# First attention's scores as two full-array passes over stacked parts, with the parts made by ScalarE and VectorE

## What is computed

```python
q = rmsnorm(q.reshape(B, S, N_HEADS, HEAD_DIM), q_gain)
k = rmsnorm(k.reshape(B, S, N_HEADS, HEAD_DIM), k_gain)
...
s = jnp.einsum('bqhd,bkhd->bhqk', qb, kb).astype(jnp.float32) * scale + bias
s = jnp.where(valid[None, None], s, NEG_INF)
p = jax.nn.softmax(s, axis=-1)
return jnp.einsum('bhqk,bkhd->bqhd', p.astype(vb.dtype), vb)
```

## Time and profile before

| | |
|---|---|
| median of three runs | 1531.12 us |
| the profiled execution's own time | 1531.12 us |
| its span, first to last instruction | 1529.3 us |
| TensorE busy | 1508.3 us (99%) |
| VectorE, ScalarE, GpSimd busy | 744.7, 578.6, 125.0 us |
| granted TensorE clock, mean | 0.999 |

### The profile page before, as it was taken

One profiled execution on the slowest core, in us unless ns is written; L12 is line 12 of the kernel. 1 busy time (PEld: TensorE's weight loads), 2 busy tenths in 40 slices (PEclk: granted clock), 3 DMA queues, 4 the chain that ended last, 5 costly groups with the idle time before them and its releaser, 6 DMA issues.

```text
span 1529.3 us, 18943 instructions
## 1 busy us (share of the span) xinstructions
PE 1508.3 (99%) x7006; PEld 1233.0 (81%) x7006; DVE 744.7 (49%) x1068; ACT 578.6 (38%) x941; POOL 125.0 (8%) x102
## 2 busy tenths in 40 slices
PE   8999999999999999999999999999999999999998
PEld 7888888887885688888888887887788888888886
DVE  5444433347345655444323456676557542244434
ACT  5323221224325533322212255666745443124322
POOL 0000000002005120000000024256000000000000
PEclk9999999999999999999999999999999999999999
DMA  6333353334221133333333334520233332233222
GB/s 188 97 99 95 98 138 100 97 97 122 86 83 47 56 110 92 96 99 95 98 97 97 96 97 112 178 83 29 83 100 111 107 96 96 97 96 96 96 97 97
DMA packets 247833, 151.19 MB, mean 99 GB/s; under 512 B 18128, under 2 KB 230752, under 8 KB 247520
## 3 DMA queue, kind: packets, MB, share of 16 engines
q1 hardware_dynamic: 234432, 143.67, 31.9%
q10 hardware_dynamic: 13344, 6.75, 1.6%
HBM read 144.10 MB, written 5.78 MB: 98 GB/s over the span
## 4 chain that ended last, share of the span: by engine, by line
PE 91%; DVE 3%; ACT 3%; issue 1%; DMA 1%; SPq 0%; DVEq 0%; ACTq 0%
PE bank L389 29%; PE bank L393 28%; PE bank L392 28%; DVE w_low L1196 1%; PE bank L2151 1%; PE bank L2203 1%; DMA region_f<-in_x 1%; PE bank L2162 1%; ACT w_high L655 0%; PE bank L2375 0%; PE bank L2090 0%; DVE region L1540 0%; DMA rope_w<-rope_y 0%; PE bank L2235 0%; PE bank L2214 0%
## 5 line engine op out<-in xcount | busy, mean ns | idle before, releaser
L389 PE MATMUL bank<-region,w_high 128*128 128x512 f32 (+2 forms) x1492 | 585.3, 392 | 4.9 <-DVE w_low L1196 1.4
L393 PE MATMUL bank<-region,w_low 128*128 128x512 f32 (+2 forms) x1492 | 579.4, 388 | 0.0
L392 PE MATMUL bank<-region,w_high 128*128 128x512 f32 (+2 forms) x1492 | 579.0, 388 | 0.0
L1196 DVE TENSOR_TENSOR w_low<-w_raw,w_high 128x1024 fp32r<-128x1024 f32 (+1 forms) x259 | 334.0, 1295 | 149.9 <-ACT w_high L655 145.9
L655 ACT CAST w_high<-w_raw 128x1024 fp32r<-128x1024 f32 (+1 forms) x259 | 265.8, 1027 | 257.6 <-DMA w_raw<-in_ffn_w_down 107.2
L389 PEld LDWEIGHTS bank<-region,w_high 128*128 128x128 f32 (+1 forms) x1492 | 279.6, 187 | 65.6 <-DVE w_low L1196 3.8
L393 PEld LDWEIGHTS bank<-region,w_low 128*128 128x128 f32 (+1 forms) x1492 | 279.5, 187 | 59.2
L392 PEld LDWEIGHTS bank<-region,w_high 128*128 128x128 f32 (+1 forms) x1492 | 279.7, 187 | 56.0
L389 PE MATMUL bank<-w_high,region 128*128 128x512 f32 x416 | 164.3, 395 | 2.4 <-ACT x L978 1.5
L393 PE MATMUL bank<-w_high,region 128*128 128x512 f32 x416 | 162.2, 390 | 0.0
L392 PE MATMUL bank<-w_low,region 128*128 128x512 f32 x416 | 161.9, 389 | 0.0
(11 more groups left out here) (265 smaller groups left out, 1188.8 us busy)
## 6 DMA issues: line engine op xcount, KB each, us to landing
w_raw<-in_ffn_w_down SPq DMA_DIRECT2D x48, 512.0 KB, 3.9
w_raw<-in_ffn_w_gate SPq DMA_DIRECT2D x44, 512.0 KB, 3.8
w_raw<-in_ffn_w_up SPq DMA_DIRECT2D x44, 512.0 KB, 3.8
w_raw<-in_w_in SPq DMA_DIRECT2D x40, 512.0 KB, 3.9
w_raw<-in_w_up SPq DMA_DIRECT2D x32, 512.0 KB, 4.0
w_raw<-in_w_down SPq DMA_DIRECT2D x32, 512.0 KB, 3.3
w_raw<-in_w_out SPq DMA_DIRECT2D x16, 512.0 KB, 3.9
region_f<-in_x SPq DMA_DIRECT2D x4, 512.0 KB, 7.5
```

Source lines behind the costliest of these rows:

```text
L389: mm = pe.matmul(out, a_hi, b_hi, start=start, stop=False)
L392: pe.matmul(out, a_hi, b_lo, start=False, stop=False)
L393: return pe.matmul(out, a_lo, b_hi, start=False, stop=stop)
L1196: last = dve.tensor_tensor(piece(w_low[b % RING]), piece(w_raw[b % RING]), piece(w_high[b % RING]).bitcast(F32), ALU.subtract)
```

## The change

The scores of a window are computed by two fp32r passes for each head, each over all 128 rows. The stationary operand is a stacked query tile: the high part of the head's queries in its own 64 partitions (HOME) and the low part in the other 64 (OTHER). The first pass multiplies it with a tile that holds the high part of the keys in both halves, the second with a tile that holds the low part of the keys in the home half and zeros in the other. For each pair of heads ScalarE makes 6 copies of 64x512 (2 of queries, 4 of keys), VectorE 4 subtractions of 64x512, GpSimd 2 memsets of 64x512. Pairs 2 and 3 use the same tiles as 0 and 1, and their high parts wait for the scores of the pair two before. GpSimd's four memsets stand ahead of its pool work. The head norms are spread in the order 0, 4, 1, 5, 2, 6, 3, 7. The semaphores of the second block's parts are shared with the new ones and counted on.

```diff
@@ ScalarE, after the casts of the value blocks
+            def a_query_parts(p):
+                act.wait_ge(qk_full_ready, 2 * p + 1)
+                if p >= 2:
+                    act.wait_ge(a_score, 8 * (p - 1))
+                for c in range(2):
+                    last = act.copy(a_query(p, c)[HOME[c], :], over[1][HOME[c], p, :])
+                last.then_inc(query_hi, 1)
+            def a_key_parts(p):
+                act.wait_ge(qk_full_ready, 2 * p + 2)
+                if p >= 2:
+                    act.wait_ge(a_score, 8 * (p - 1))
+                for c in range(2):
+                    act.copy(a_key(p, c)[HOME[c], :], over[1][HOME[c], 4 + p, :])
+                    last = act.copy(a_key(p, c)[OTHER[c], :], over[1][HOME[c], 4 + p, :])
+                last.then_inc(key_hi, 1)
+            for p in range(2):
+                a_query_parts(p)
+                a_key_parts(p)
@@ ScalarE, loop, after the exponentials and before the copy of sums, pooled_hi and split_hi
+                if w in (4, 8):
+                    a_query_parts(w // 4 + 1)
+                if w in (5, 9):
+                    a_key_parts(w // 4 + 1)
@@ VectorE, head norms
+                j = HEAD_ORDER[i]
                 dve.wait_ge(h_bc, i + 1)
-                dve.scalar_tensor_tensor(over[1][:, i, :], qk_raw[:, i, :], qk_gain[:, i // 4:i // 4 + 1],
+                dve.scalar_tensor_tensor(over[1][:, j, :], qk_raw[:, j, :], qk_gain[:, j // 4:j // 4 + 1],
@@ VectorE, after the value tiles
+            def query_low_parts(p):
+                dve.wait_ge(query_hi, p + 1)
+                for c in range(2):
+                    last = dve.tensor_tensor(a_query(p, c)[OTHER[c], :], over[1][HOME[c], p, :],
+                                             a_query(p, c)[HOME[c], :].bitcast(F32), ALU.subtract)
+                last.then_inc(query_lo, 1)
+            def a_key_low_parts(p):
+                dve.wait_ge(key_hi, p + 1)
...
+                for c in range(2):
+                    last = dve.tensor_tensor(a_key_low(p, c)[HOME[c], :], over[1][HOME[c], 4 + p, :],
+                                             a_key(p, c)[HOME[c], :].bitcast(F32), ALU.subtract)
+                last.then_inc(key_lo, 1)
+            query_low_parts(0)
+            a_key_low_parts(0)
             u_tile(0, bank[5])
             for w in range(2 * HEADS):
                 p, q = divmod(w, TT)
+                if w in (1, 5, 9):
+                    query_low_parts(w // 4 + 1)
+                if w in (2, 6, 10):
+                    a_key_low_parts(w // 4 + 1)
@@ GpSimd, after the sum of squares
+            for p in range(2):
+                if p == 1:
+                    pool.wait_ge(qk_full_ready, 8)
+                for c in range(2):
...
+                    pool.memset(a_key_low(p, c)[OTHER[c], :].bitcast(F32), 0.0).then_inc(pads_in, 1)
@@ TensorE
-                pe.matmul(bank[6 + i % 2][:], head_select[:, P * i:P * (i + 1)], head_rows[:], start=True, stop=True).then_inc(h_bc, 1)
+                j = HEAD_ORDER[i]
+                pe.matmul(bank[6 + i % 2][:], head_select[:, P * j:P * (j + 1)], head_rows[:], start=True, stop=True).then_inc(h_bc, 1)
...
+                if q == 0:
+                    pe.wait_ge(query_lo, p + 1)
+                    pe.wait_ge(key_lo, p + 1)
+                    pe.wait_ge(pads_in, min(2 * p + 2, 4))
...
-                    pe.matmul(bank[4 + c][:, 0:n], over[1][rows_, p, q * P:(q + 1) * P], over[1][rows_, 4 + p, 0:n],
-                              start=True, stop=True).then_inc(a_score, 1)
+                    queries = a_query(p, c)[:, q * P:(q + 1) * P]
+                    pe.matmul(bank[4 + c][:, 0:n], queries, a_key(p, c)[:, 0:n], start=True, stop=False)
+                    pe.matmul(bank[4 + c][:, 0:n], queries, a_key_low(p, c)[:, 0:n], start=False, stop=True).then_inc(a_score, 1)
```

More of the change, by code:

```diff
@@ L121 @@
 SQ, _ = numbered([("m1", 8), ("f2", 8), ("m2", 16)])
+PARTS, _ = numbered([("a", 4), ("d", 4)])
+PADS, _ = numbered([("a", 4), ("d", 8)])
 SPREAD, _ = numbered([("f1", 1), ("m1", 1), ("f2", 1), ("m2", 1)])
@@ L340, in build, with a_query, a_key, a_key_low @@
         CONV_ORDER = (0, 2, 1, 3)
+        HEAD_ORDER = (0, 4, 1, 5, 2, 6, 3, 7)
+        A_QUERY = (((2, 4), (2, 5)), ((1, 9), (1, 10)))
+        A_KEY = (((2, 6), (2, 7)), ((1, 11), (1, 15)))
+        A_KEY_LOW = (((2, 16), (2, 17)), ((2, 13), (2, 14)))
+        def a_query(p, c):
+            return d_place(A_QUERY, p % 2, c)
+        def a_key(p, c):
+            return d_place(A_KEY, p % 2, c)
+        def a_key_low(p, c):
+            return d_place(A_KEY_LOW, p % 2, c)
         mv_plain = over[2][:].rearrange("p a b -> p (a b)")[:, 0:TT * MH * MV].rearrange("p (k h c) -> p k h c", k=TT, h=MH)
@@ L515, in build @@
         mv_ready = sem("mv_ready")
-        e_query_hi, e_query_lo, e_key_hi, e_key_lo, e_padded = (sem("d_" + n) for n in (
+        query_hi, query_lo, key_hi, key_lo, pads_in = (sem(n) for n in (
             "query_hi", "query_lo", "key_hi", "key_lo", "key_pads_zero"))
@@ L923, in d_query_hi @@
                     last = act.copy(d_query(h, c)[HOME[c], :], over[1][HOME[c], h, :])
-                last.then_inc(e_query_hi, 1)
+                last.then_inc(query_hi, 1)
             def d_key_hi(h):
@@ L929, in d_key_hi @@
                 if h == 2:
-                    act.wait_ge(e_key_lo, 2)
+                    act.wait_ge(key_lo, PARTS["d"] + 2)
                 if h == 3:
-                    act.wait_ge(e_query_lo, DH)
+                    act.wait_ge(query_lo, PARTS["d"] + DH)
                 for c in range(2):
@@ L935, in d_key_hi @@
                     last = act.copy(d_key(h, c)[OTHER[c], :], over[1][HOME[c], 4 + h, :])
-                last.then_inc(e_key_hi, 1)
+                last.then_inc(key_hi, 1)
             for i in range(8):
@@ L1536, in d_query_lo @@
             def d_query_lo(h):
-                dve.wait_ge(e_query_hi, h + 1)
+                dve.wait_ge(query_hi, PARTS["d"] + h + 1)
                 for c in range(2):
@@ L1541, in d_query_lo @@
                                              d_query(h, c)[HOME[c], :].bitcast(F32), ALU.subtract)
-                last.then_inc(e_query_lo, 1)
+                last.then_inc(query_lo, 1)
             def d_key_lo(h):
-                dve.wait_ge(e_key_hi, h + 1)
+                dve.wait_ge(key_hi, PARTS["d"] + h + 1)
                 if h == 2:
@@ L1549, in d_key_lo @@
                 if h == 3:
-                    dve.wait_ge(e_key_lo, 3)
+                    dve.wait_ge(key_lo, PARTS["d"] + 3)
                 for c in range(2):
@@ L1553, in d_key_lo @@
                                              d_key(h, c)[HOME[c], :].bitcast(F32), ALU.subtract)
-                last.then_inc(e_key_lo, 1)
+                last.then_inc(key_lo, 1)
             for i in range(6, 8):
@@ L1866, in _ @@
             sum_squares("m1")
+            pool.wait_ge(sq_added, SQ["m1"] + DT)
+            for p in range(2):
+                if p == 1:
+                    pool.wait_ge(qk_full_ready, 8)
+                for c in range(2):
+                    if p or c:
+                        pool.wait_ge(pads_in, 2 * p + c)
+                    pool.memset(a_key_low(p, c)[OTHER[c], :].bitcast(F32), 0.0).then_inc(pads_in, 1)
+            pool.wait_ge(pads_in, 4)
             for j in range(4):
@@ L1896, in _ @@
                 if h == 3:
-                    pool.wait_ge(e_key_lo, 3)
+                    pool.wait_ge(key_lo, PARTS["d"] + 3)
                 for c in range(2):
                     if h or c:
-                        pool.wait_ge(e_padded, 2 * h + c)
-                    pool.memset(d_key_low(h, c)[OTHER[c], :].bitcast(F32), 0.0).then_inc(e_padded, 1)
+                        pool.wait_ge(pads_in, PADS["d"] + 2 * h + c)
+                    pool.memset(d_key_low(h, c)[OTHER[c], :].bitcast(F32), 0.0).then_inc(pads_in, 1)
             def convolve(i):
@@ L2315, in d_scores @@
                 if q == 0 and c == 0:
-                    pe.wait_ge(e_query_lo, h + 1)
-                    pe.wait_ge(e_key_lo, h + 1)
-                    pe.wait_ge(e_padded, 2 * h + 2)
+                    pe.wait_ge(query_lo, PARTS["d"] + h + 1)
+                    pe.wait_ge(key_lo, PARTS["d"] + h + 1)
+                    pe.wait_ge(pads_in, PADS["d"] + 2 * h + 2)
                 if u >= 2:
```

5 lines of the change are left out of this document (2 added, 3 removed).

## The result

The kernel after takes **1550.11 us** (median of 4 runs, 1547.01 to 1551.12), the kernel before 1531.13 on the same chip: ratio 1.0118 with a 95% interval of 1.0106 to 1.0129 (ratios are given so below), 19.0 us slower. The forecast was 1541.0 with a range to 1546. The sign and the places of the waits were right; GpSimd's blocking and TensorE's clock were priced far too low. The profiled execution is the shortest of the four, 1547.01 us at a mean granted clock of 0.995; the other three had 0.991 to 0.993. So the trace explains 15.9 us of the 19.0.

What follows compares the result with a forecast made beforehand. The prediction took TensorE to bound the kernel (busy 99%, 91% of the chain). Loop waits of 11.0 plus 0.5 for GpSimd less 1.6 gained gave +9.9 us on 1531.12, so 1541.0, range 1534.5 to 1546.

Steps and rivals of the forecast that it cites:

- 1: scores of window 3: Before window 3's scores: VectorE's two key subtractions delay window 2's minima, with no cover; +1.4 us.
- 2: sums of window 5: Spreading the sums, window 5: query copies and subtractions lengthen the chain by 2.64 us against cover 0.85; +1.8 us.
- 3: scores of window 7: Before window 7's scores: ScalarE's four key copies delay its pool cast, then VectorE's subtractions and minima; dearest, +3.3 us.
- 4: sums of window 9: Spreading the sums, window 9: chain again 2.64 us longer against a cover of about 0.45; +2.2 us.
- TensorE's own gain: Score passes in the attention loop: new form gains 0.4 us a pair, 1.6 for four; bounds 1.0 and 2.6.
- Ahead of the loop: Parts made before the loop's first scores: cost nothing, with a cover of 1.3 us.
- The six places: Waits of TensorE at windows 3, 5, 7, 9, 11 and 12 from parts made inside the loop; 11.0 us together.
- I take 0.5 in all: Subtractions of windows 1 and 5 slowed beside GpSimd's additions: 0 to 0.6 us each of four, 0.5 taken in all.
- The rival: GpSimd blocks VectorE: four subtractions lose about a whole addition each, 4.4 us instead of 0.5, 1544.9; chance 0.10.
- The clock: Rival: clock falls in window 7's stall, next 3 to 5 us of TensorE work take twice as long, 1545; chance 0.10.
- Hiding: Rival: new ScalarE and VectorE work fits their idle time in the loop, leaving only TensorE's gain, 1529.5; chance 0.10.
- cheaper instructions: Rival: loop copies and subtractions overlap at some 0.5 and 0.6 us and covers recover, 1536.8; chance 0.15.

Runs made afterwards that it cites:

- e6_moved2: Changed kernel with its new copies and subtractions placed where engines idled, and pair 0's low part and the last key subtraction moved later; 1529.53 us.
- e10: Changed kernel without GpSimd's running sums, with 10, 10, 20 and 10 extra TensorE transposes fitted into four waits; 1541.13 us, ratio 1.0066.
- e1: Changed kernel with 26, 18, 12 and 16 extra TensorE transposes into a free bank during four waits; 1546.51 us, ratio 1.0104.
- e8_place1: Changed kernel with pair 1's four subtractions ahead of the loop instead of at the heads of windows 1 and 2; 1544.96 us, ratio 1.0083.
- e2_nopool: Changed kernel with GpSimd's running sums left out, a scaling of 8 columns in their place; 1543.54 us, ratio 1.0079.
- e3_short: Changed kernel with the copies and subtractions of pairs 2 and 3 cut to 8 of 512 columns; 1537.20 us, ratio 1.0042.

## Why the prediction was wrong, step by step

The array's work is the same in all these kernels but the one before, so the time from one window's first score pass to the next one's, less the same in e6_moved2, prices each place. All from the profiled executions, in us:

| place of the forecast | forecast | order alone (e10) | with GpSimd's sums (e1) | and the clock (after) |
|---|---|---|---|---|
| 1: scores of window 3 | 1.4 | 1.45 | 3.87 | 3.87 |
| (window 4, no place) | 0 | -0.01 | 0.00 | 1.04 |
| 2: sums of window 5 | 1.8 | 1.67 | 3.10 | 3.96 |
| 3: scores of window 7 | 3.3 | 3.54 | 3.54 | 2.66 |
| 4: sums of window 9 | 2.2 | 1.53 | 2.75 | 3.39 |
| 5: scores of window 11 | 1.5 | 1.81 | 1.81 | 1.16 |
| 6: window 12 and behind its scores | 0.8 | 1.23 | 1.23 | 1.23 |
| all of the loop | 11.0 | 11.35 | 16.45 | 17.44 |

The last line has 0.14 us more than the six places and window 4 together; it lies behind the scores of window 7.

- **TensorE's own gain, -1.6: right in sum.** Before less e6_moved2 is 1.83 us in the same count, 1.7 between the medians. By pair it is 0.91, 0.42, 0.26 and 0.24, not 0.4 each. The scores of 128 keys were read too dear, 0.46 where they take 0.39 (475.53 to 475.92 in the kernel after).
- **Ahead of the loop, 0: right**, and the cover of 1.3 was 1.5. e8_place1 shows what its end costs.
- **The six places, 11.0: right in their order and cause; that the sums agree so well (11.35) is partly luck.** Each is within 0.7 of e10_hold_fitted, but that kernel also lacks the 1.62 us by which GpSimd already lengthened three `split_lo` in the kernel before. With that time put back at places 1, 2 and 4 they are 1.5, 2.4 and 2.4, each of the six is dearer than forecast, and the loop comes to about 13.0 (an estimate from these traces): some 2 us too little in the forecast. (Place 4's rows give a cover of 0.51 where I wrote about 0.45, a tenth at most.) The count through ScalarE's queue for place 3 held: 3.3 against 3.54. The alternative in which each cover is whole again after a stall (9.2) is not what happened.
- **GpSimd, "I take 0.5 in all": the step that failed.** Measured: 16.45 less 11.35, 5.1 us in the loop, 5.4 between the medians of e1 and e10. Of it 1.6 stood in the forecast's rows already, so the term that was put at 0.5 is about 3.5. All of it falls on the three places that have VectorE work beside GpSimd's additions: 2.4, 1.4 and 1.2. At place 1, 0.9 of the 2.4 come from window 1, whose subtractions were thought to be free: their delay passes through the exponentials and ScalarE's cast to `split_lo`, which starts 2.03 us after window 2's scores in e1_hold and 1.12 in e10_hold_fitted. The row that I chose by, a `split_lo` of 1.32 beside a scaling, is true of a one-input GpSimd instruction; the subtractions of windows 1, 2 and 5 meet two-input ones. The rival had this mechanism at 4.4 and got 0.10, on the strength of that one row. The trace of before had a second row against it, a `split_lo` of 128x512 beside two-input additions, 1.53 us where a VectorE subtraction of that shape takes 0.69:

```profile
489.42 1.53 DVE L1196 TENSOR_TENSOR w_low<-w_raw,w_high 128x512 fp32r<-128x512 f32 x1
```

- **The clock, left to a rival and put at nothing in the sum: failed too.** It came true on top of GpSimd's share, not instead of it. It cost 1.0 us in the trace and 3.6 between the medians of the kernel after and e1. Without GpSimd's sums it fell once, at place 3 as the rival had it, and cost 2.4 us (e2_nopool less e10_hold_fitted), so by these medians 2.4 of the 3.6 are a cost of their own and only some 1.2 need both causes. What I held against it, that the stall is shorter than the idle time at the end of the kernel in which the clock stayed full, took one fall for a bound. In the kernel after the clock fell when TensorE had been idle for 2.7 us of the wait of 3.01, and in e8_place1 behind a wait of 1.96.
- **Hiding and cheaper instructions: refuted** by the first row of the table and by 0.62 and 0.69 us for a copy and a subtraction.

The sum by the measured terms: 9.95 (order, with TensorE's gain in it), 5.4 and 3.6 make 19.0, which is what the medians differ by. It must come out so, since each term is the step from one kernel to the next; the terms depend on the order in which the causes are taken out. My two dear rivals stood at 1544.9 and 1545 each for itself; both together, 1540.5 without the 0.5, plus 4.4 and 4, would have been 1548.9.

Two rules of the Trainium skill bear on this. VectorE and GpSimd: two subtractions of 64x512 took 2.31 us beside GpSimd's additions, 1.39 without them (e2_nopool); the `split_lo` of window 2 took 1.61 beside the one-input scaling and 1.23 without. "SBUF — State Buffer", section "Who interferes with whom", has a two-input VectorE instruction and any GpSimd instruction that reads SBUF exclude each other for the whole instruction. The subtractions agree; the `split_lo` doesn't, since it ended at 468.05, 0.19 after a scaling that ran from 466.36 to 467.86, and can't have waited for its end. The clock: in the kernel after it was at half rate behind waits of 3.75, 3.01 and 2.68 us and full behind 1.97; it was full behind 1.60 in e2_nopool, and fell behind 1.96 in e8_place1. "TensorE: Matmul & The Clock Gate", section "What's actually happening", calls the throttled state the default that activity lifts, and the transposes of e1_hold agree: with them in the same gaps the profiled clock was 1.00.

**What stays open.** Why the three executions of the kernel after without a trace had a lower clock than the profiled one, and where their further 3 us lie, isn't shown; that they lie in the clock is inferred from their mean (0.991 to 0.993) and from e1_hold. Since the executions of e1_hold without a trace weren't at full clock either (0.996 to 0.998), a part of the 5.4 us between e1_hold and e10_hold_fitted may be the clock's; the traces alone give GpSimd 5.1. Whether the `split_lo` beside a scaling shares time with it or is slowed in another way wasn't tried.

## What to carry to other kernels

Work moved into a tuned loop is priced by who queues behind it, not by the idle share of its engine: the same twelve copies and twelve subtractions for later pairs cost 20.6 us at the head of the windows and nothing behind the cast and the minima (one pair's subtractions went ahead of the loop). Ask of each VectorE instruction with two inputs which GpSimd instruction runs beside it, and price a whole one if that has two inputs too. When a forecast makes TensorE wait 2 to 4 us, as here, price the clock in the sum (here 2.4 to 3.6 us between medians); dear mechanisms that can come true together belong in one case too, not only in separate rivals. And read covers and durations with the same engines at work as in the experiment that is to confirm them.

## What the hardware showed unexpectedly

- A subtraction of 64 rows by 8 columns takes VectorE about 0.17 us (two in 0.33) against 0.69 for 512 columns, and a copy of 8 columns takes ScalarE 0.20 against 0.62: a floor of a quarter to a third stays when the columns are cut 64 times. Beside GpSimd's sums two of the short subtractions took 0.77 and 1.06 us: 0.4 and 0.7 are lost by two instructions that last 0.33, so the loss doesn't shrink in step with the instructions that lose it.
- A `split_lo` of 128x512, 0.69 us alone (e2_nopool), takes 1.52 beside GpSimd's additions in the kernel after (at 500.89, with an addition of 1.37 from 500.50): most of an addition is lost, and in a row of groups it looks like a slow instruction.
- The clock does not follow from the length of one wait. It stayed full behind a wait of 1.97 us in the kernel after and fell to half behind one of 1.96 in e8_place1 (at 463.0, 1.4 us after TensorE had started again). In e8_place1 the spread sums behind waits of 2.99 and 2.67 us take 1.09 us, full rate (over the 5 us around the first the granted clock is 1.00, around the second 0.69: it fell behind the sums); in the kernel after, behind 3.01 and 2.68, they take 1.98 and 1.74. In e3_short the pass behind 3.75 us is at full rate (0.50), and window 4 comes 1.30 us late for work done at half rate after it.
- The wait that the trace shows before an instruction shrinks when the clock fell earlier: window 7 waits 1.97 us in the kernel after and 3.37 in e8_place1 and e2_nopool, with the same cause.
